# Block two's projections of a two-block transformer kernel in another chunk order: values first, then queries, keys, gates

## The reference, cut to what matters

```python
hn = rms_norm_2(h, mix_norm_pre)
proj = hn @ w_in                       # 1024 x 3272 columns
rq, rk, rv, rg, aq, ak, av, iq, ik, iw = split_columns(proj)   # rq, rk, rv, rg, aq: 512 columns each
rq, rk = apply_rope(rq), apply_rope(rk)                        # rotation by position, 8 heads of 64
ret_out = retention(rq, rk, rv, rg)    # per chunk of 128 rows: (q k^T * decay) v + q state; state += k^T v
aq, ak, iq, ik = (apply_rope(a) for a in (aq, ak, iq, ik))
# for every query row: score all earlier keys by relu(iq ik^T) iw, keep the 256 best, softmax attention over those
att_out = dsa_attention(aq, ak, av, iq, ik, iw)
h = h + rms_norm_2(concatenate([ret_out, att_out]) @ w_out, mix_norm_post)
```

## Time and profile before

| | value |
|---|---|
| median of three runs | 2885.61 us (2882.16 to 2888.72) |
| profiled execution, its own time | 2880.87 us |
| its span in the trace | 2879.1 us |
| mean granted PE clock | 0.982 |
| PE busy | 2754.2 us, 96% |
| DVE, ACT, POOL busy | 62%, 43%, 41% |
| the changed chunks (queries, keys, values) | 1612.3 to 1775.5 us of the span |
| the gate chunk | 1775.5 to 1863 us |

### The profile page before, as it was taken

The page is one execution under the profiler, slowest core; times in us unless marked ns, Lnnn a source line. Parts: engine busy times, 40 slices in busy tenths (PEclk is TensorE's granted clock), DMA queues, the critical chain, the costliest instruction groups (busy, mean ns, idle before and its releaser), DMA issues. The chain is left out here.

```text
span 2879.1 us, 38826 instructions
## 1 busy us (share of the span) xinstructions
PE 2754.2 (96%) x13656; PEld 2259.5 (78%) x13656; DVE 1789.7 (62%) x2684; ACT 1246.6 (43%) x2267; POOL 1187.1 (41%) x838
## 2 busy tenths in 40 slices
PE   6999999999999999999998789989999999999998
PEld 6877788887788888888887567867778888887886
DVE  6758757323676666622846888775567778776153
ACT  6226544101533333323544667537553444443243
POOL 2011223334634444544642233531173466665454
PEclk8999999999999999999999899999999999999999
DMA  7431112323421222255530113100242222124452
GB/s 260 156 116 30 30 45 64 106 66 103 139 90 57 87 87 87 73 176 161 186 107 8 37 52 117 52 1 9 81 147 66 81 73 86 67 80 168 150 191 90
DMA packets 176237, 272.35 MB, mean 95 GB/s; under 512 B 13145, under 2 KB 105561, under 8 KB 176089
## 3 DMA queue, kind: packets, MB, share of 16 engines
q1 hardware_dynamic: 176088, 270.39, 28.3%
HBM read 224.21 MB, written 46.14 MB: 94 GB/s over the span
## 5 line engine op out<-in xcount | busy, mean ns | idle before, releaser
L2082 POOL TENSOR_TENSOR sb_out_lo<-sb_out_raw,sb_out_hi 128x512 fp32r<-128x512 f32 (+1 forms) x174 | 312.1, 1801 | 312.7 <-ACT sb_out_hi L2069 312.6
L133 PE MATMUL psum<-sb_out_hi,sb_a_hi 128*128 128x512 f32 x912 | 357.8, 392 | 5.5 <-ACT sb_junk L2293 4.4
L135 PE MATMUL psum<-sb_out_hi,sb_a_lo 128*128 128x512 f32 x912 | 355.1, 389 | 0.0
L134 PE MATMUL psum<-sb_out_lo,sb_a_hi 128*128 128x512 f32 x912 | 355.0, 389 | 0.0
L1555 POOL TENSOR_TENSOR sb_pair_lo<-sb_pair_sum,sb_pair_hi 128x512 fp32r<-128x512 f32 x180 | 236.8, 1327 | 269.6 <-ACT sb_pair_hi L1699 269.6
L133 PE MATMUL psum<-sb_h_hi,sb_w_hi 128*128 128x512 f32 x640 | 256.8, 401 | 2.9 <-DVE sb_h_lo L2229 2.4
L134 PE MATMUL psum<-sb_h_lo,sb_w_hi 128*128 128x512 f32 x640 | 249.6, 390 | 0.0
L135 PE MATMUL psum<-sb_h_hi,sb_w_lo 128*128 128x512 f32 x640 | 249.6, 390 | 0.0
L134 PE MATMUL psum<-sb_h_lo,sb_pair_hi 128*128 128x512 f32 x576 | 224.1, 389 | 0.0
L133 PE MATMUL psum<-sb_h_hi,sb_pair_hi 128*128 128x512 f32 x576 | 224.1, 389 | 0.0
L135 PE MATMUL psum<-sb_h_hi,sb_pair_lo 128*128 128x512 f32 x576 | 224.1, 389 | 0.0
(11 more groups left out here) (488 smaller groups left out, 6370.2 us busy)
## 6 DMA issues: line engine op xcount, KB each, us to landing
act_kept<-sb_gate_up SPq DMA_DIRECT2D x40, 512.0 KB, 2.8
sb_pairs_raw<-in_w_up SPq DMA_DIRECT2D x18, 1024.0 KB, 5.3
sb_late_w<-in_w_ada SPq DMA_DIRECT2D x32, 512.0 KB, 4.9
sb_w_raw<-in_w_in SPq DMA_DIRECT2D x54, 256.0 KB, 3.4
sb_out_raw<-in_w_ffn_down SPq DMA_DIRECT2D x44, 256.0 KB, 3.1
sb_out_raw<-in_w_down SPq DMA_DIRECT2D x44, 256.0 KB, 2.8
sb_act_ring<-act_kept SPq DMA_DIRECT2D x40, 256.0 KB, 4.0
sb_act_late<-act_kept SPq DMA_DIRECT2D x40, 256.0 KB, 4.0
```

What stands on the lines that cost most here:

```text
L133: nc.tensor.matmul(out, stationary.hi, moving.hi, start=start, stop=False)
L134: nc.tensor.matmul(out, stationary.hi, moving.lo, start=False, stop=False)
L135: return nc.tensor.matmul(out, stationary.lo, moving.hi, start=False, stop=stop)
L2082: self.nc.gpsimd.tensor_tensor(w.lo, raw, w.hi.bitcast(F32), ALU.subtract).then_inc(self.w_lo, 1)
```

## The change

The chunks are now done in the order values, queries, keys, gates, attention queries. Value items are n = 0 to 7, query items 8 to 15, key items 16 to 23; gates stay 24 to 31. With it:

- `STEPS`: no step at n = 0 and 1, one at n = 2 to 7, two at n = 8, one at n = 9 to 31. From n = 9 on, a step has the n that it had before.
- `cut_rows` on ACT moves from ahead of item 0's work to n = 2, behind the copies of value rows 0 and 1.
- SP issues the weights k = 4 to 7 of the next chunk ahead of the spill of item n - 1, no longer behind it.
- The transpose of query row n - 2 stands behind item n; rows 6 and 7 are transposed within and behind the pair of the first two key items. ACT's `rows_out` follows by the same distance.
- At the start of the query and key chunks PE waits for the second item's bank only after three steps of the first; at the gate chunk it waits for both banks at the start as before.
- The weights of the queries are split beside the value chunk, those of the gates beside the keys.
- The retention's load waits for the key row's spill before the value row's.

```diff
-            sp.dma_start(first_raw[:, :, :], wv[:, 0:2, OFF_RET:OFF_RET + W]).then_inc(first_got, 16)
+            sp.dma_start(first_raw[:, :, :], wv[:, 0:2, OFF_RET + 1024:OFF_RET + 1024 + W]).then_inc(first_got, 16)
...
-Q_, K_, V_, G_, A_ = range(5)
-STEPS = [max(n - 1, 0) for n in range(4 * TB)] + [BITS] * 11
+V_, Q_, K_, G_, A_ = range(5)
+STEPS_IN = [0, 0] + [1] * 6 + [2] + [1] * (3 * TB - 1) + [0] * (TB + 1)
+STEPS = [sum(STEPS_IN[:n]) for n in range(len(STEPS_IN) + 1)]
...
-    starts = [OFF_RET, OFF_RET + 512, OFF_RET + 1024, OFF_RET + 1536, OFF_AQ]
+    starts = [OFF_RET + 1024, OFF_RET, OFF_RET + 512, OFF_RET + 1536, OFF_AQ]
...
# row_slot_free (a row buffer is free when the row two before it is used)
-            if c == Q_:
+            if c == Q_ and t >= 2:
                 eng.wait_ge(turned, place[c, t - 2] + 1)
...
             else:
-                eng.wait_ge(spilled[m % 2], 16 * ((m - 2 - TB) // 2 + 1))
+                rows_spilled = m // 2 if c in (V_, Q_) else (TB + t) // 2 if c == K_ else TB
+                eng.wait_ge(spilled[m % 2], 16 * rows_spilled)
...
# SP
-                weights(0, 2, KD)
+                weights(V_, 2, KD)
                 for n in range(N + 1):
+                    if n < N and items[n][1] == TB - 1 and items[n][0] + 1 < 5:
+                        weights(items[n][0] + 1, 4, KD)
                     if n and items[n - 1][0] in (K_, V_):
...
-                    if (c, t) == (V_, 5) or c == G_ and 0 < t < TB - 1:
+                    if (c, t) == (K_, 5) or c == G_ and 0 < t < TB - 1:
...
-                    if c + 1 < 5 and t == TB - 1:
-                        weights(c + 1, 4, KD)
...
# PE
                 def bank_free(n):
                     last = n - 3 if items[n][0] != A_ else n - 2
                     if n >= 3:
-                        if items[last][0] in (V_, G_):
+                        if items[last][0] == V_:
+                            pe.wait_ge(act_read, last + 1)
+                        elif items[last][0] == G_:
                             pe.wait_ge(act_read, last - 2 * TB + 1)
...
-                    if c == Q_ or t > 1 or (c, t) == (A_, 0):
+                    if c == V_ or t > 1 or (c, t) == (A_, 0):
                         bank_free(n)
                     elif t == 0:
                         bank_free(n)
-                        bank_free(n + 1)
+                        if c == G_:
+                            bank_free(n + 1)
...
-                    elif c == Q_ and t == 2:
-                        steps(n, 0, 4)
-                        turn_rows(0).then_inc(turned, 1)
-                        steps(n, 4, KD)
...
                     elif t == 0:
-                        pair(n, 0, KD)
-                    if n > 1 and items[n - 1][0] == Q_:
-                        turn_free(items[n - 1])
-                        turn_rows(n - 1).then_inc(turned, 1)
+                        steps(n, 0, 3)
+                        bank_free(n + 1)
+                        steps(n + 1, 0, 3)
+                        pair(n, 3, 5)
+                        if c == K_:
+                            turn_free(items[n - 2])
+                            turn_rows(n - 2).then_inc(turned, 1)
+                        pair(n, 5, KD)
+                        if c == K_:
+                            turn_free(items[n - 1])
+                            turn_rows(n - 1).then_inc(turned, 1)
+                    if c == Q_ and t > 1:
+                        turn_free(items[n - 2])
+                        turn_rows(n - 2).then_inc(turned, 1)
...
# POOL
-                lows(Q_, 2)
+                lows(V_, 2)
+                lows(Q_)
                 for c in (Q_, K_):
                     for t in range(TB - 2):
                         add_turned(c * TB + t)
...
-                lows(G_)
...
# ACT
-                highs(0, 2, KD)
-                top.cut_rows(act)
+                highs(V_, 2, KD)
...
+                    if n == 2:
+                        top.cut_rows(act)
                     for s in range(STEPS[n], STEPS[n + 1]):
                         top.count(act, s)
...
-                    if (c, t) == (V_, TB - 1):
+                    if (c, t) == (K_, TB - 1):
                         turn_done((K_, 0))
                         ret.keys_out().then_inc(turn_out, 1)
...
-                    if 0 < n <= N and items[n - 1][0] == Q_:
-                        rows_out(n - 1)
+                    if n > 1 and items[n - 2][0] == Q_:
+                        rows_out(n - 2)
```

More of the change, by code:

```diff
@@ L3013, in load @@
             sp.wait_ge(self.o_done, r - 1)
+        sp.wait_ge(spilled[r % 2], 16 * ((TB + r) // 2 + 1))
+        sp.dma_start(self.kr[:, r % 2, :], self.k_d[0, r * P:(r + 1) * P, :]).then_inc(self.kr_got[r % 2], 16)
         sp.wait_ge(spilled[r % 2], 16 * (r // 2 + 1))
-        sp.dma_start(self.kr[:, r % 2, :], self.k_d[0, r * P:(r + 1) * P, :]).then_inc(self.kr_got[r % 2], 16)
-        sp.wait_ge(spilled[r % 2], 16 * ((TB + r) // 2 + 1))
         sp.dma_start(self.vr[:, r % 2, :], self.v_d[0, r * P:(r + 1) * P, :]).then_inc(self.vr_got[r % 2], 16)
@@ L3122, in scaled @@
         self.nc.vector.tensor_tensor(gr, gr, self.ms[:, r % 2, :].unsqueeze(2).to_broadcast([P, RH, HD]), ALU.mult).then_inc(self.rows_ready, 1)
-Q_, K_, V_, G_, A_ = range(5)
-STEPS = [max(n - 1, 0) for n in range(4 * TB)] + [BITS] * 11
+V_, Q_, K_, G_, A_ = range(5)
+STEPS_IN = [0, 0] + [1] * 6 + [2] + [1] * (3 * TB - 1) + [0] * (TB + 1)
+STEPS = [sum(STEPS_IN[:n]) for n in range(len(STEPS_IN) + 1)]
+assert STEPS[-1] == BITS
 class Sparse:
@@ L3390, in _ @@
                             sp.wait_ge(act_read, t + 1)
-                        sp.dma_start(spill[c - K_][0, t * P:(t + 1) * P, :], rr[:, rows_no[n - 1] % 2, :]).then_inc(spilled[rows_no[n - 1] % 2], 16)
+                        sp.dma_start(spill[c == V_][0, t * P:(t + 1) * P, :], rr[:, rows_no[n - 1] % 2, :]).then_inc(spilled[rows_no[n - 1] % 2], 16)
                     if n == N:
@@ L3394, in _ @@
                     c, t = items[n]
-                    if (c, t) == (V_, 5) or c == G_ and 0 < t < TB - 1:
-                        if c == V_:
+                    if (c, t) == (K_, 5) or c == G_ and 0 < t < TB - 1:
+                        if c == K_:
                             sp.wait_ge(top.masked, TOP_STEPS * len(SUMMED) + 1)
-                        for r in (0, 1) if c == V_ else (t + 1,):
+                        for r in (0, 1) if c == K_ else (t + 1,):
                             ret.load(sp, r, spilled)
@@ L3413, in steps @@
                             pe.wait_ge(lo_done, c * KD + k + 1)
-                        done = multiply(nc, core.ps[:, bank(n), :], h.tile(k, t), first_w[:, k] if c == Q_ and k < 2 else w[:, k], k == 0, k == KD - 1)
+                        done = multiply(nc, core.ps[:, bank(n), :], h.tile(k, t), first_w[:, k] if c == V_ and k < 2 else w[:, k], k == 0, k == KD - 1)
                         if t == TB - 1:
@@ L3527, in _ @@
                             attending(n, t)
-                    elif c == Q_ and t == 0:
+                    elif c == V_ and t == 0:
                         steps(0, 0, 2)
```

## The result

Twenty runs of the changed kernel have a median of 2888.3 us (2885.07 to 2893.28), twenty of the kernel before 2883.49 us. The ratio is 1.0015, with a 95% interval of 1.0009 to 1.0021: slower by 4.3 us (2.6 to 6.1; the ratio times the time before). Forecast were +4.7 us, as a time 2890.3 us, with a range of 2878 to 2897.

What follows compares the result with a forecast made beforehand. PE was busy 96% of the span, with DVE's search and rotations forecast to gate the gate chunk: 1.7 us later start plus 3.0 us slow clock, +4.7 us on 2885.61, giving 2890.3 us, range 2878 to 2897.

Steps and rivals of the forecast that it cites:

- parts 1, 4 and 5: Values: PE's 4.46 us wait goes; first query transpose: PE waits 2.1 us; queries to keys: PE waits 3.0 us.
- parts 2 and 3: Search starts 3.2 us later, no PE wait; steps beside values at ACT's 4.60 us pace, row 8 rotated at 1678.0.
- parts 5, 6 and 8: DVE cycles beside POOL's tiles: 9.5 us for rotation 14, 9.7 for rotation 15, 9.7 plus 0.9 for rotation 22.
- Part 6: Loads ahead of spills: ACT's 6.72 us weight wait goes; rotation 15's cycle taken as 9.7 us, at most 10.3.
- part 8: Keys to gates: rotation 22's cycle 9.7 plus 0.9 us; PE idle 11.8 us, then 3.0 us lost to slow clock.
- part 7: Keys with float32 steps: six DVE cycles of 6.67 us; PE waits about 1 us before items 21, 22 and 23.
- rival E: In e_spill_first: loads ahead of spills keep the change from being worse; undoing them costs 3 us or more, +0.25% against before.
- Short contended cycles: Rival: the three transitions beside POOL's tiles cost 10.6 us less, gates start 8.9 us earlier, total 2877; chance 0.17.
- Spill over into the gates: Rival: late rotation 23 delays the retention's first product and DVE's state update, +9 to +12 us, 2896; chance 0.15.
- Absorbed in early attention: Rival: early attention's 16.8 idle us, hanging on DVE, ACT and POOL, take in the shift, +0, 2885.6; chance 0.13.

Runs made afterwards that it cites:

- e_cut_first: The changed kernel with ACT's cuts of the scores ahead of the copies of value rows 0 and 1 again; ratio to before 1.0014, key transpose at 165.9 us.
- e_no_lows: The changed kernel without POOL's subtractions for the weights of keys and gates (16 tiles), everything signalled as before; ratio to before 0.9972, key transpose at 155.1 us.
- e_spill_first: The changed kernel with the loads of the next chunk's last four weight tiles behind the spill again; ratio to before 1.0021.
- e_old_seven: The old chunk order with the change's other parts and one search step moved from n = 7 to n = 17; ratio to before 0.9987.
- e_old_one_later: The old chunk order with the change's other parts and one search step moved from n = 15 to n = 20; ratio to before 0.9986.

## Why the prediction was right

**Where PE waits (parts 1, 4 and 5).** No wait within the values; 2.62 us at the first query transpose (2.1 forecast); 2.96 us in the key pair (3.0). The rotations of the queries came as forecast: counted from the first matmul, row 8 is rotated at 65.4 us (1681.5 less 1616.1; forecast 1678.0 less 1612.3, 65.7).

**The search chain at the start (parts 2 and 3)** reached the right time by a reason that is half right. The search started 18.9 us after the first matmul (forecast 19.4), and the pace of 4.60 us held. But the sum took every later time from that start, and e_cut_first shows that 2.9 us of it could go with no effect. The chain starts anew at PE's last value item; that the two coincided within a microsecond was luck.

**Contended cycles (parts 5, 6 and 8).** The first took 9.6 us (9.5 forecast), the second 10.43 (9.7, with an upper end of 10.3), the third 11.13 (10.6). Part 6 chose 9.7 for a float32 step beside four tiles, below the upper end that takes over the whole loss of the bfloat16 cycle, and part 8 built on the 9.7. That term was too small. Against e_no_lows the tiles cost DVE's cycle nearly the same beside both kinds of comparison: 3.8 us for the first (9.63 and 5.83), 3.7 for the second (10.43 and 6.69), 4.0 for the third (11.13 and 7.12). The second cycle is 0.7 us longer than forecast and the third 0.5, and that is why the key transpose is later than forecast by 1.1 us (+2.8, not +1.7).

**Keys with float32 steps (part 7).** 6.70 us a cycle (6.67), waits of 0.84 us (1), the last wait 12.04 us (11.8).

**The clock.** Forecast 3.0 us lost behind the wait at the gates, measured 1.8: the slow stretch ended at about 1785.9, 3.8 us after the wait, though the wait was longer than the one of 8.44 us with 5.9 us behind it. The 1.6 us that the trace gives back in the gates were not forecast; as said above, they may belong to the one execution of the kernel before. So of the sum of +4.7 the terms are +2.8 (for +1.7) and +1.8 (for +3.0): one was 1.1 us too small, the other 1.2 us too large, and that they cancel is luck. Their sum is +4.6, with the gates' -1.6 it is the trace's +3.1 (but for rounding), and the runs have +4.3 (2.6 to 6.1), which agrees with either. The path, DVE's chain that ends at rotation 22 and PE's wait for it, was right.

**Part 6, loads.** The sum has no term for them, and the trace of e_spill_first bears that out (165.4 us for 166.0 at the key transpose); its runs alone would allow a gain of rival E's size.

**The rivals.** Short contended cycles: not so, but their price was: 10.6 us forecast for three short cycles, 11.0 us measured when they were made short. Spill over into the gates: not in the changed kernel, where no second long wait follows the key transpose; the kernels with moved steps did lose time in the gates, but at another wait, for DVE's product L3101. Absorbed in early attention: no, the shift passes through (from the 0.94 us wait at the end of the gates to the output projection it is 205.3 us in the changed kernel, before 205.2).

## What to carry to other kernels

Count a moved part at its new neighbours: with the rotations directly ahead of a pair that waits for them, each microsecond of steps and of contention beside them was added to DVE's chain, and PE waited 12 us at its end. Where PE asks for the banks of two items at once, its wait is two of DVE's cycles less one item of its own (17.8 - 5.8 us here). Look for the places where the chain is tied to the other engine again, as a lead does not pass them. Try the parts of a change one by one: here the transposes moved two items back and the pairs' later bank wait gained 0.2%, and the chunk order they came with lost 0.34%.

## What was not expected of the hardware

- DVE's comparisons and POOL's subtractions cost each other time, beside float32 as beside bfloat16. Three float32 comparisons took 4.54 and 4.86 us (1.88 alone), three bfloat16 ones 3.88 us (1.18 alone): 2.7 to 3.0 us more in each. POOL's four tiles took 5.62 and 6.17 us, where four beside bfloat16 comparisons took 5.38. "SBUF — State Buffer" of the Trainium skill, section "Who interferes with whom", has the second to issue wait for the whole of the first where the DVE operation is in a two-port mode; no run shows the mode of the masks. The runs agree with such waits: DVE's masks and POOL's tiles seem to take turns, one of each in some 1.6 us (4.86 / 3).
- A longer wait was not followed by a longer slow stretch of PE: 3.8 us behind 12.04 us, 5.9 us behind 8.44 us, but 10.2 us behind 2.47 us in e_old_seven and e_old_one_later. A wait of 1.66 to 1.69 us at the same place of the program was followed by one in the profiled execution of the kernel before (0.60) and by none in that of the changed kernel (1.00).
